# In-projection blocks under the recurrence's steps, modulation at each eighth block, scores one head ahead, buffers at whole 128-byte lines

## What is computed

```python
def even_mixer(hl, hc, w_in, w_out, ...):
    al, rl, kl, vl, wdl, adl, gl = split_even(hl @ w_in)       # the in-projection, 6400 columns
    ac, rc, kc, vc, wdc, adc, gc = split_even(hc @ w_in)
    for d, reverse in enumerate((False, True)):
        in_c = rwkv_dir_inputs(rc, kc, vc, ...)
        in_l = rwkv_dir_inputs(rl, kl, vl, ...)
        s_ctx, y_c = wkv7_scan(s0, in_c, reverse)              # the recurrence
        _, y_l = wkv7_scan(s_ctx, in_l, reverse)
...
def first_block(...):
    for l in range(DEPTH):
        shift_l, scale_l, gate_l = jnp.split((sc @ mod_w[l] + mod_b[l])[:, None, :], 3, axis=-1)
        hl = xl * (1.0 + scale_l) + shift_l
...
def attention(q, k, v):
    s = jnp.einsum('bqhgd,bkhd->bhgqk', q, k) * (HEAD_DIM ** -0.5)
    p = jax.nn.softmax(s, axis=-1)
    return jnp.einsum('bhgqk,bkhd->bqhgd', p, v)
```

## Time and profile before

| | before |
|---|---|
| median of 3 runs | 3887.4 us (3885.5 to 3891.88) |
| the profiled execution | 3897.59 us, its span 3895.7 us |
| TensorE busy | 3588.6 us |
| VectorE, ScalarE, GpSimd busy | 2037.8, 1540.8, 249.2 us |
| mean granted clock of TensorE | 0.963 |
| recurrence | about 180 to 1463 us of the span |
| pooling, out-projection, norms | 1463 to 1860 us |
| attention | 1860 to 2062 us |
| rest of the program | 2062 us to the end |

### The profile page before, as it was taken

The page is one execution under the profiler, slowest core; times in us unless marked ns, Lnnn a source line. Parts: engine busy times, 40 slices in busy tenths (PEclk is TensorE's granted clock), DMA queues, the critical chain, the costliest instruction groups (busy, mean ns, idle before and its releaser), DMA issues. The chain is left out here.

```text
span 3895.7 us, 71193 instructions
## 1 busy us (share of the span) xinstructions
PE 3588.6 (92%) x31388; PEld 2940.9 (75%) x31388; DVE 2037.8 (52%) x3540; ACT 1540.8 (40%) x2599; POOL 249.2 (6%) x295
## 2 busy tenths in 40 slices
PE   6889889999898998989989799989999999999998
PEld 3567666767676676767678688847989799999877
DVE  1454454544445447674565546755544455555444
ACT  2333333333333333354444444425433444444433
POOL 0001111011111113002000000110000000000000
PEclk8899999999999999999999899999999999999999
DMA  9423323242433406443234454324553545555554
GB/s 361 148 78 96 110 86 116 70 127 71 119 109 96 127 31 244 141 141 108 87 97 163 146 162 141 126 96 140 183 191 130 169 159 183 183 184 184 194 178 157
DMA packets 349474, 548.59 MB, mean 141 GB/s; under 512 B 11724, under 2 KB 119916, under 8 KB 346988
## 3 DMA queue, kind: packets, MB, share of 16 engines
q1 hardware_dynamic: 346716, 538.78, 42.5%
q10 hardware_dynamic: 2448, 5.24, 0.4%
HBM read 535.86 MB, written 8.13 MB: 140 GB/s over the span
## 5 line engine op out<-in xcount | busy, mean ns | idle before, releaser
L302 PE MATMUL lane<-r,r 128*128 128x256 f32 (+1 forms) x8520 | 1506.5, 325 | 45.6 <-DVE r L260 38.8
L302 PE MATMUL bank<-r,r 128*128 128x512 f32 (+2 forms) x6360 | 1400.9, 358 | 38.0 <-DVE r L260 28.1
L260 DVE TENSOR_TENSOR r<-ring,r 128x1024 fp32r<-128x1024 f32 x770 | 939.7, 1227 | 935.5 <-ACT r L299 934.2
L302 PEld LDWEIGHTS lane<-r,r 128*128 128x128 f32 x8520 | 1263.2, 190 | 219.1 <-DVE r L260 46.0
L302 PEld LDWEIGHTS bank<-r,r 128*128 128x128 f32 x6360 | 1044.2, 193 | 255.7 <-issue 55.3
L299 ACT ACTIVATE r<-ring 128x1024 fp32r<-128x1024 f32 x770 | 808.1, 1056 | 970.1 <-PE lane L302 570.1
L302 PE MATMUL lane<-arena 64*64 64x64 f32 (+5 forms) x12940 | 653.3, 257 | 68.0 <-DVE arena L260 18.4
L302 PEld LDWEIGHTS lane<-arena 64*64 64x64 f32 (+3 forms) x12940 | 489.2, 141 | 237.0 <-issue 111.3
L299 ACT ACTIVATE arena<-lane 128x256 f32<-128x256 f32 (+3 forms) x578 | 249.1, 451 | 551.7 <-PE lane L302 449.8
L260 DVE TENSOR_TENSOR arena<-arena 128x256 f32<-128x256 f32 (+7 forms) x568 | 259.3, 488 | 36.3 <-ACT arena L299 14.8
L271 DVE COPY arena<-lane 128x256 f32<-128x256 f32 (+3 forms) x366 | 131.8, 362 | 272.5 <-PE lane L302 255.6
(11 more groups left out here) (93 smaller groups left out, 1266.8 us busy)
## 6 DMA issues: line engine op xcount, KB each, us to landing
ring<-in_w_gate_up SPq DMA_DIRECT2D x88, 1024.0 KB, 5.0
ring<-in_mod_w SPq DMA_DIRECT2D x73, 1024.0 KB, 5.3
ring<-in_ev_w_in SPq DMA_DIRECT2D x44, 1024.0 KB, 8.9
ring<-in_w_down SPq DMA_DIRECT2D x44, 1024.0 KB, 5.1
ring<-in_od_w_in SPq DMA_DIRECT2D x40, 1024.0 KB, 5.1
ring<-in_w_in SPq DMA_DIRECT2D x40, 1024.0 KB, 5.1
ring<-in_w_xkv SPq DMA_DIRECT2D x32, 1024.0 KB, 5.4
ring<-in_ev_w_out SPq DMA_DIRECT2D x28, 1024.0 KB, 5.2
```

The source lines that it names most:

```text
L260: return Nothing() if self.e is None else self.e.tensor_tensor(o, a, b, op)
L302: return Nothing() if self.e is None else self.e.matmul(o, l, r, start=start, stop=stop)
```

## The change

It has four parts.

1. `FILL` holds more blocks for nine steps (`shift`, `kk_sum`, `keys`, `turn_AV`, `P_LR`, `KR1`, `double0`, `gn_sum`, `read_out`): a unit's sum goes from 41 to 50.5. No block is left for a bulk; a unit has 44 to 46 blocks (36 before), the last 35 (28 before). `made` follows the last `rkv_in` column in place of `gate_in`, and `load_lora` goes behind it.
2. The modulation has no share of its own (`MOD_SHARE` is gone): one `mod` stands directly behind each unit of 8 blocks, through `due`, with `mod_row` in the same turn.
3. In the attention the scores of head h + 1 are issued before the transposes of head h, and the last two steps of the softmax are a step of their own, `soften`.
4. All buffers are rounded up to whole lines of 32 words. Before, the ring began at byte 29728 of a partition and the arena at 54304, both 32 behind a multiple of 128; after, 30080 and 54656, both multiples of 128. The arena has 112 words less. `TAIL` holds for the last unit alone.

```diff
-FILL = {"shift": 4, "kk_sum": 6, "keys": 4.5, "turn_AV": 2, "P_LR": 1, "KR0": 1, "KR1": 1, "solve": 0.5, "GH": 1,
-        "QY": 1, "state0": 2, "state1": 2, "state2": 2, "state3": 2, "centre": 3, "gn_sum": 6, "read_out": 2}
-MOD_SHARE = 0.125
+FILL = {"shift": 5.5, "kk_sum": 7.5, "keys": 6, "turn_AV": 3, "P_LR": 1.5, "KR0": 1, "KR1": 1.5, "double0": 0.5, "solve": 0.5,
+        "GH": 1, "QY": 1, "state0": 2, "state1": 2, "state2": 2, "state3": 2, "centre": 3, "gn_sum": 6.5, "read_out": 3.5}
+LINE = 32
...
+def whole(n):
+
+    return (n + LINE - 1) // LINE * LINE
...
-        return ctx.enter_context(nc.sbuf_tensor(name, [P, n], F32))
+        return ctx.enter_context(nc.sbuf_tensor(name, [P, whole(n)], F32))
...
-            yield False
             if k0 == KT - 4:
                 step("mod_row", l, g, b)
-                yield False
+            yield
+            if k0 == KT - 4:
                 step("mod_col", l, g, bank(mod_turn))
-                yield False
+                yield
...
-                if sm.kind == "gate_in":
+                if sm.args[1:] == (2,):
                     step("load_lora", hp)
...
-            for end in ev_blocks(u, ev_turn):
-                if end and hp is not None and u.blocks[0][0].kind == "gate_in":
+            for j, end in enumerate(ev_blocks(u, ev_turn)):
+                if end and hp is not None and u.blocks[0][0].kind == "rkv_in" and u.blocks[0][0].args[1] == 2:
                     made[0] = hp
-                yield end
+                yield j == len(u.blocks) - 1
...
-    share = [0.0, 0.0]
+    share, due = [0.0], [False]
...
             share[0] -= 1
-            share[1] += MOD_SHARE
-            i = 0
-            if share[1] >= 1:
-                share[1] -= 1
-                i = len(sources) - 1
-            end = next(sources[i], None)
-            if end is None:
+            i = len(sources) - 1 if due[0] else 0
+            due[0] = False
+            end = next(sources[i], "none")
+            if end == "none":
                 sources.pop(i)
-            if end:
-                return
+            elif end:
+                due[0] = True
...
+    LAST_UNIT = 23 * (2 * HPS - 1) + LAG
...
-        if ended and x in TAIL:
+        if ended and x in TAIL and rounds > LAST_UNIT:
...
+    def score(h):
+        if h < 16 and h // 4 in ready and h not in scored:
+            scored.add(h)
+            for qt in range(2):
+                step("scores", h // 4, h, qt, bank(aux))
...
         for h in range(4 * n, 4 * n + 4):
-            for qt in range(2):
-                step("scores", n, h, qt, bank(aux))
+            if h not in scored:
+                score(h)
+                yield ATT[0]
+            soften(h)
+            score(h + 1)
             yield ATT[0]
             for kt2 in range(2):
                 step("p_turned", h, kt2, bank(aux))
+            soften(h + 1)
             yield ATT[1]
```

More of the change, by code:

```diff
@@ L463, in layout @@
     M.pair = [a[:, 0:1024].rearrange("p (b n) -> p b n", b=2) for a in lanes]
-    M.cm = sb("cm", cm_np.shape[1])[:]
-    M.vec = sb("vec", NVEC)[:]
-    M.vx = sb("vx", 16)[:]
+    M.cm = sb("cm", cm_np.shape[1])[:, 0:cm_np.shape[1]]
+    M.vec = sb("vec", NVEC)[:, 0:NVEC]
+    M.vx = sb("vx", 16)[:, 0:16]
     M.smod = sb("smod", KT * 32)[:]
@@ L470, in layout @@
     M.modv = sb("modv", 192)[:]
-    M.omu = sb("omu", 48)[:]
-    M.gnb = sb("gnb", 8)[:]
+    M.omu = sb("omu", 48)[:, 0:48]
+    M.gnb = sb("gnb", 8)[:, 0:8]
     M.small = sb("small", 64)[:]
@@ L475, in layout @@
     M.ring = sb("ring", RING * PIECE)[:]
-    free_words = 53140 - (cm_np.shape[1] + NVEC + 16 + KT * 32 + 512 + 192 + 56 + 128 + RING * PIECE)
-    free_words = free_words // 8 * 8
-    arena_at = (nc.sbuf_base + 31) // 32 * 32
+    fixed = [cm_np.shape[1], NVEC, 16, KT * 32, 512, 192, 48, 8, 64, 64, RING * PIECE]
+    free_words = (53140 - sum(whole(n) for n in fixed)) // LINE * LINE
+    arena_at = nc.sbuf_base
+    assert arena_at % (4 * LINE) == 0
     arena = sb("arena", free_words)
@@ L1161, in order_of_work, with soften @@
     ready = set()
+    scored = set()
+    def score(h):
[3 more added lines that the diff above has]
+                step("scores", h // 4, h, qt, bank(aux))
+    def soften(h):
+        if h in scored and h not in softened:
+            softened.add(h)
+            step("soften", h)
+    softened = set()
     def attend(n):
         for h in range(4 * n, 4 * n + 4):
-            for qt in range(2):
-                step("scores", n, h, qt, bank(aux))
+            if h not in scored:
[3 more added lines that the diff above has]
+            score(h + 1)
             yield ATT[0]
@@ L2588, in scores, with soften @@
         i = (2 * h + qt) % 4
-        if h >= 2:
-            v.wait_ge(*at("pS_read", h - 2))
-        soft_rows(b, 512, M.pS[i], float(P) ** -0.5, M.st1[:, 32 + 4 * i:36 + 4 * i], ("pS", h, qt))
+        st = M.st1[:, 32 + 4 * i:36 + 4 * i]
+        full(b)
+        v.maximum(st[:, 0:1], M.bank[b[0]]).then_inc(*v.n())
+        own()
+        v.ts(st[:, 1:2], st[:, 0:1], -float(P) ** -0.5, None, MUL).then_inc(*v.n(("top", "pS", h, qt)))
+    def soften(h):
+        for qt in range(2):
+            i = (2 * h + qt) % 4
+            st = M.st1[:, 32 + 4 * i:36 + 4 * i]
+            v.wait_ge(*at("exp", "pS", h, qt))
+            v.recip(st[:, 3:4], st[:, 2:3]).then_inc(*v.n())
+            own()
+            v.ts(M.pS[i], M.pS[i], st[:, 3:4], None, MUL).then_inc(*v.n(("pS", h, qt)))
     def values(n, h, b):
@@ L3012, in vector_program @@
         read_out, combine, first_done, split_w, split, pool, pool_mix, pool_done, gate_diag, add_first, ctx_done,
-        norm0, norm0_q, h1, h1_done, to_q, to_k, to_v, k_rows, v_rows, q_rows, hn_square, hn_gain, hn_turn, hn_turned, hn_done, scores,
+        norm0, norm0_q, h1, h1_done, to_q, to_k, to_v, k_rows, v_rows, q_rows, hn_square, hn_gain, hn_turn, hn_turned, hn_done, scores, soften,
         values, gate_heads, add_second, attended, norm1, rms, rms_turned, vg_in, gla_ready, gl_gate, gl_decay, gl_spread, gl_keys,
```

## The result

The changed kernel takes 4022.97 us, the median of four runs (4015.73 to 4028.29), against 3887.16 before: a ratio of 1.0346, 95% interval 1.0326 to 1.0366, 136 us slower. Forecast were 3994 us and a range of 3835 to 4060.

A forecast was written before the change was run, and what follows sets the result against it. TensorE, busy 92%, was taken to bound the kernel through its work, idle time and clock. Stalls +114, clock +40, cover −30 and scores ahead −17 summed to +107, taking the median 3887.4 to 3994 us, range 3835 to 4060.

The forecast's parts named there:

- Stalls behind the modulation: Recurrence: columns requested directly behind a mod stall TensorE at 30 places, 168 us against 54, +114; this forecast's chance 0.72.
- The rule itself: Recurrence: a TensorE stall is release time less work in hand, mean 12.0 less 6.4 us at 30 places.
- the place that I had priced: Recurrence: one place behind a mod with 4.0 us of TensorE work in hand, so a stall of 8 us.
- The 20 us that the rule didn't give: Recurrence before: part of 53.9 us idle behind landings, where the rule gives no stall; left out of the sum.
- The clock: Recurrence: 20 more long stalls each cost 2 us of TensorE work at half clock, +40, bounds 20 and 61.
- Less where TensorE would have waited anyway: Clock term: discount from 2.3 to 3.0 us lost per stall, to the 2 us taken.
- Cover: Recurrence: blocks moved out of the bulks cover the lanes' 55 us of short waits, −30, bounds 0 and −50.
- Scores ahead: Attention: next head's scores hide TensorE's 18.0 us wait for the softmax's last scaling, −17, bounds 0 to −18.
- Aligned buffers: r-views and ring start at another multiple of 128 bytes; nothing expected to change, taken as 0.
- No row shows it: Alignment term: no profile row shows an aligned fp32r operand beside one that isn't.
- Rival B: Alignment speeds fp32r matmuls by 10.6 and 22 ns, at most 230 us; with 200 the time is 3794; chance 0.08.
- Rivals A and C: Recurrence: A, stalls don't grow, cover wins, 3840 us, chance 0.15; C, half the stalls are covered, 3890, chance 0.05.

The follow-up runs named there:

- e1: Changed kernel with the ev_w_in column put ahead of the next mod_w piece in SP's queue; 3782.4 us, ratio 0.9747 to the kernel before.
- e2: Changed kernel with mod chosen by a share of its own again (0.108 of the turns); 3885.8 us, ratio 1.0009 to the kernel before.
- e5: Kernel before with every later ev_w_in column ahead of the mod_w piece SP waits on; 3830 us, ratio 0.9851.
- e7: e5 with scores ahead and aligned buffers added; 3816.5 us, ratio 0.9813 to the kernel before.
- e9: e8 with one line more, a fill stops behind a unit's last block; ratio 0.9747 to the kernel before.
- e4: Kernel before with the attention part of the change alone (scores a head ahead, soften a step); ratio 0.9959, 16 us faster.
- e6: Kernel before with the aligned buffers alone; ratio 0.9988 to the kernel before.
- e10: e1 with activations starting at 32 and split weights at 0 behind a multiple of 128 bytes; ratio 0.9741 to the kernel before.
- e11: e1 with activations starting at 0 and split weights at 64 behind a multiple of 128 bytes; 3754.6 us, ratio 0.9638 to the kernel before.
- e8: e2 with all ev_w_in columns ahead as in e5; 3823 us, ratio 0.9832 to the kernel before.
- e3: Kernel before with e1's edit, which reached only columns with no blocks between mod and column; ratio 0.9969.

## Why the prediction was right, and where it wasn't

**Stalls behind the modulation, +114.** Measured +128: 53.9 to 181.6 us, 26 pieces over 3.1 us where 27 were reckoned. e1 shows the cause, by SP's order alone, and e2 that it is the place of the `mod`. The rule itself held: 28 stalls stand behind a column that went out right behind a `mod`; from the end of the `mod` TensorE resumes after 12.5 us on average (12.0 reckoned), with 6.6 us of work in hand (6.4), and idles 166 us in all (168). At the place that I had priced it was 13.9 us and not 12, since the `rw` transfers stood between, which I had put at nothing: seven columns stand behind such a pair and go out 1.5 us after their `mod`, one of them 2.9, in place of 0.5. Most of the excess over +114 isn't the column's: 13.2 us of the 181.6, and 3.6 of the 53.9, end before the column lands, at blocks that wait for their bank. ScalarE's wait was 264.7 us, 30 times, in the forecast's 250 to 300.

**The 20 us that the rule didn't give.** I left them where they were. e5 shows that they stay when the columns are early, so they were not the column's; in the kernel after they may be partly covered by the larger fills.

**The clock, +40.** TensorE's work in the recurrence grew by 33 us (1183 to 1216), the count of instructions being the same. The clock records of the traces show 106 us at 1.2 GHz before, 253 after and 48 in e1, in 20, 36 and 9 stretches. But TensorE idles in part of that time: it works 90, 177 and 43 us of it. So 87 us more of work at the lower level cost 33, and from the kernel after to e1 134 us less gave back 65: 0.4 and 0.5 us for a microsecond worked. That is the half of the forecast, and single rows bear it out: in the kernel after a matmul of a block takes 427 ns to the next at the lower level and 231 at the higher (medians), a 128-column transpose 214 and 109. The Trainium skill's rule (TensorE: Matmul & The Clock Gate, Terms), the throttled time × (1 − K/N), would give half of all 147 us, 73, as an estimate: too much here, since it counts the time in which TensorE waits. "Less where TensorE would have waited anyway" was the right discount. The counts behind the number were off: of the kernel before's 20 stretches my count by pieces over 3.1 us found 7 (by the trace 6 are that long); 16 more came and not 20, and the 36 are 7.0 us long on average, where the 20 before were 5.3, as I took. Work lost is 2.1 us for each new one, against the 2 taken; 33 in place of 40 is mostly the count.

**Cover, −30.** Measured −20 in the kernel after (53.4 to 33.5), or −10 if the waits for the bank are counted here and not at the landings; −23 of idle and −26 us of time from e7 to e9, which differ in the fills and little else. The place of the `mod` covers the bank as well, which I hadn't seen at all: the prediction put it only on the side of losses. e9 shows that a lane's step does the same.

**Scores ahead, −17.** −10 in the stretch, −16 in the medians of e4. The 18.0 us went, but another wait grew in their place: TensorE's for VectorE's L268, from 4.9 to 10.7 us in the attention.

**Aligned buffers, 0.** The net is −5 us, so the term was right in size by luck: two effects of some 25 us each cancel. "No row shows it" was true; that nothing would come of it rested on VectorE and ScalarE and on lines of 16 bytes, and TensorE tells the starts apart by 3 to 6 ns a matmul. The Trainium skill (SBUF — State Buffer, Door 1: The DMA port swizzle) has the lines of 16 bytes; that nothing depends on a start at a multiple of them was my inference, and e6, e10 and e11, whose starts are all such multiples, show it wrong for fp32r matmuls. Rival B had the right mechanism at a fraction of its size, and half of it with the other sign.

**Sum.** Between the profiled executions: stalls +128, other idle in large and small pieces −23, clock +33, the attention −10, the middle −6, start and end −4: 118 us. So the traces are 11 us over the forecast's +107. The medians are 136 apart, 29 over it; the 18 us between are the spread of single executions and can't be given to a term. Rivals A and C, by which TensorE would have 12 or 9 us of work in hand, fall with the measured 6.6.

## What to carry to other kernels

A queue that issues in order passes its waits on: put a transfer whose buffer is already free ahead of one that waits for the engine you want to keep busy, and look at what stands in front of a late transfer before you look at its bandwidth. Moving a waiting step to a regular place can make it coincide with the same neighbour every time; some 131 us came from that here (the kernel after against e2), and one transposition in SP's list turned a kernel 136 us slower than before into one 101 us faster. Where consecutive groups share one PSUM bank, keep some other work of a microsecond between them: at such places TensorE idled 36 us without it (e8) and 9 with it (e9).

## What the runs showed of the hardware

- An fp32r matmul's pace depends on where its operands start in a partition, at steps of 32 and 64 bytes: means of 114 to 120 ns at 256 columns and 227 to 233 at 512, from the kernel before, e6, e10 and e11. Where the activations start at 32 and the weights at 96 something else moves it too, between 113 and 118 (before, e3, e4).
- At the lower of the clock's two levels a 512-column matmul of a block takes 427 ns in place of 231. In the recurrence a microsecond at 1.2 GHz cost 0.2 to 0.3 us if the time in which TensorE idles is counted (33 us for 147, and 65 for 205), and 0.4 to 0.5 of the time in which it works.
- A column of 1 MB lands 8.1 to 9.6 us after its issue when a piece of `mod_w` goes out just ahead of it (31 columns of the kernel after), and in 5.7 where none does (issued at 1478.90 us there, landed at 1484.6); the page's median of the 44 is 8.3.
